# Convolution taps of one channel group on GpSimd beside the top-k, and the rotations of queries and keys after it, in a two-block sparse-attention kernel

## The reference, cut to what matters

```
proj = einsum('bld,de->ble', h, w_in[l])
a, g, zc, q, k, v, za, qi, ki, wi = split(proj)
# convolution branch: 31 taps in each of 512 channels, one after the other
u = a * sigmoid(g);  u = depthwise_conv(u, w_dw, width 31, causal) + b_dw
y_conv = silu(layer_norm(u)) * silu(zc)
# attention branch
q, k, qi, ki = apply_rope(each)               # x*cos + shifted(x)*sin
score = sum over 8 index heads of relu(qi . ki * s) * wi, causal
idx = top_k(score, 132)                       # of 528 keys, for each row
y_attn = softmax(q . k over idx) v * silu(za)
h = layer_norm(ALPHA * h + concat(y_conv, y_attn) @ w_out[l])
```

## Time and profile before

| | us |
|---|---|
| median of 3 runs | 1114.37 (1112.88 to 1114.47) |
| the profiled execution | 1111.81 |
| its span in the trace | 1110.0 |
| PE busy | 1021.1 (92%) |
| DVE busy | 697.7 (63%) |
| ACT busy | 581.6 (52%) |
| POOL busy | 130.8 (12%) |

### The profile page before, as it was taken

How to read it: one execution, slowest core, us unless ns; L and a number is a source line. 1 busy time by engine, 2 the same in 40 slices (tenths; PEclk the granted TensorE clock), 3 DMA queues, 4 the chain that set the end, 5 groups by cost and what they waited for, 6 DMA issues and landing times.

```text
span 1110.0 us, 16657 instructions
## 1 busy us (share of the span) xinstructions
PE 1021.1 (92%) x6484; PEld 868.8 (78%) x6484; DVE 697.7 (63%) x1553; ACT 581.6 (52%) x938; POOL 130.8 (12%) x185
## 2 busy tenths in 40 slices
PE   7998899778999899989989898969999999999997
PEld 7987898766677799879887666758888778877885
DVE  3999999785465559999978755562841333332522
ACT  6584781546543548458437544462484555565331
POOL 0000100101121200010001121124300000000001
PEclk9998999889899999989999989999999999999999
DMA  8775674454300767547528523295767644547661
GB/s 287 182 175 172 156 184 115 125 103 114 66 12 18 210 136 195 123 118 173 114 83 188 136 50 89 68 236 117 224 153 175 167 119 110 138 96 167 164 157 76
DMA packets 23822, 152.36 MB, mean 137 GB/s; under 512 B 2865, under 2 KB 3377, under 8 KB 6849
## 3 DMA queue, kind: packets, MB, share of 16 engines
q0 software_dynamic: 9648, 68.75, 33.4%
q1 hardware_dynamic: 14096, 82.55, 20.9%
HBM read 149.20 MB, written 2.10 MB: 136 GB/s over the span
## 4 chain that ended last, share of the span: by engine, by line
PE 77%; ACT 9%; DVE 6%; DMA 5%; issue 3%; POOL 0%; POOLq 0%; DVEq 0%; SPq 0%; ACTq 0%
PE psum_B L1176 20%; PE psum_A L1176 14%; PE psum_B L1209 9%; PE psum_A L1209 9%; PE psum_A L1330 6%; DMA w_lo<-in_weights 3%; DVE conv_acc L1626 2%; PE psum_C L1232 2%; ACT w_hi L613 2%; PE psum_B L1288 2%; PE psum_A L1542 2%; ACT w_lo L614 2%; PE psum_B L1330 2%; PE psum_B L1542 2%; DMA w_raw<-in_weights 2%
## 5 line engine op out<-in xcount | busy, mean ns | idle before, releaser
L1626 DVE SCALAR_TENSOR_TENSOR conv_acc<-u,vec,conv_acc 128x528 f32<-128x528 f32 (+1 forms) x240 | 173.4, 758 | 3.2
L1176 PE MATMUL psum_B<-x_hi,w_hi 128*128 128x264 f32 (+3 forms) x512 | 147.4, 327 | 10.7 <-ACT shifted L668 5.8
L1176 PE MATMUL psum_B<-x_lo,w_hi 128*128 128x264 f32 (+3 forms) x512 | 144.0, 320 | 0.0
L1176 PE MATMUL psum_B<-x_hi,w_lo 128*128 128x264 f32 (+3 forms) x512 | 143.4, 319 | 0.0
L1011 POOL DMA_DIRECT2D w_lo<-in_weights x67 | 59.3, 886 | 677.0 <-ACT w_lo L614 677.0
L613 ACT ACTIVATE w_hi<-w_raw 128x2048 fp32r<-128x2048 f32 (+2 forms) x87 | 129.5, 1489 | 14.3 <-DMA w_raw<-in_weights 13.9
L614 ACT ACTIVATE w_lo<-w_raw 128x2048 fp32r<-128x2048 f32 (+2 forms) x87 | 128.9, 1481 | 0.0
L1176 PE MATMUL psum_A<-x_hi,w_hi 128*128 128x264 f32 (+2 forms) x496 | 119.2, 298 | 8.2 <-DVE za L1743 4.0
L1176 PE MATMUL psum_A<-x_lo,w_hi 128*128 128x264 f32 (+2 forms) x496 | 116.8, 293 | 0.0
L1176 PE MATMUL psum_A<-x_hi,w_lo 128*128 128x264 f32 (+2 forms) x496 | 116.6, 293 | 0.0
L1176 PEld LDWEIGHTS psum_B<-x_hi,w_hi 128*128 128x128 f32 (+1 forms) x512 | 90.3, 192 | 20.0 <-issue 14.0
(11 more groups left out here) (324 smaller groups left out, 2098.0 us busy)
## 6 DMA issues: line engine op xcount, KB each, us to landing
w_raw<-in_weights SPq DMA_DIRECT2D x67, 1024.0 KB, 5.3
w_lo<-in_weights POOLq DMA_DIRECT2D x65, 1024.0 KB, 8.2
x_first<-in_x_t SPq DMA_DIRECT2D x4, 528.0 KB, 7.0
h<-in_x SPq DMA_DIRECT2D x1, 2048.0 KB, 9.8
out<-h SPq DMA_DIRECT2D x4, 512.0 KB, 2.6
post_ln_g<-in_post_ln_g SPq DMA_DIRECT2D x2, 512.0 KB, 4.2
post_ln_b<-in_post_ln_b SPq DMA_DIRECT2D x2, 512.0 KB, 5.6
w_raw<-in_weights SPq DMA_DIRECT2D x2, 288.0 KB, 5.3
```

Of the source, the lines that this page charges most:

```text
L1176: mm = pe.matmul(ps[0:cols, i, 0:b - a], w[wp][:, kt, at:at + cols], x[xp][:, kt, a:b], start=(kt == 0 and wp + xp == 0), stop=(kt == KD - ...
L1626: got = dve.scalar_tensor_tensor(dst, src, w, dst, ALU.mult, ALU.add)
```

## The change

27 of the 31 taps of group 2 go from DVE to POOL (`POOL_TAPS`). [...] They stand in POOL's order behind the selects on the scores: 3 taps at once, 5 behind the issue that follows `q` 0, 5 behind that of `q` 2, 5 behind that of `k` 0, 3 behind that of `k` 2 and 6 behind that of `v` 0. The third attention item's masked logits (L1723, `i == 2`) wait for the last of them, because they overwrite `e[2]`.

DVE keeps 97 taps: 54 before the top-k (37, then 4, 5, 5 and 3 in the index rounds), 43 with the attention items. Group 3 is no longer interleaved with group 2, but for its last four taps. The top-k runs through without the rotations, and behind the masks DVE rotates `q` 0, `k` 0, `q` 1, `k` 1, ... `k` 3. The shift buffers and ACT's waits for them stay as they were.

```diff
--- before.py
+++ after.py
@@ -219,15 +219,18 @@
     1: ((0, ("zc", 0)), (2, ("zc", 2)), (4, ("wo", 0, 0)), (6, ("wo", 1, 0)), (12, ("wo", 0, 1)), (14, ("wo", 1, 1))),
 }
 
+POOL_TAP_COUNT = 27
+POOL_TAPS = [(2, tap) for tap in range(POOL_TAP_COUNT)]
+POOL_TAPS_AFTER = {("q", 0): (3, 8), ("q", 2): (8, 13), ("k", 0): (13, 18), ("k", 2): (18, 21), ("v", 0): (21, 27)}
+
 TAPS = [(0, tap) for tap in range(11)]
 for _i in range(TAP_COUNT - 11):
     TAPS += [(0, 11 + _i), (1, _i)]
 TAPS += [(1, tap) for tap in range(TAP_COUNT - 11, TAP_COUNT)]
-TAPS += [(2, tap) for tap in range(15)]
-for _i in range(TAP_COUNT - 15):
-    TAPS += [(2, 15 + _i), (3, _i)]
-TAPS += [(3, tap) for tap in range(TAP_COUNT - 15, TAP_COUNT)]
-TAPS_AHEAD = 77
+TAPS += [(3, tap) for tap in range(TAP_COUNT - 4)]
+for _i in range(4):
+    TAPS += [(2, POOL_TAP_COUNT + _i), (3, POOL_TAP_COUNT + _i)]
+TAPS_AHEAD = 54
 TAPS_PER_ITEM = 4
 
 
@@ -493,6 +496,7 @@
         small_made = signal("small_made")
         u_made = signal("u_made")
         tap_done = signal("tap_done")
+        pool_tap_done = signal("pool_tap_done")
         rope_cos = signal("rope_cos")
         rope_sin = signal("rope_sin")
         rope_made = signal("rope_made")
@@ -519,6 +523,10 @@
                 return y_made.sem, y_made.at((use[0], "attn", use[2]))
             by = dve_took if use[1] in TAKEN_BY_DVE else act_took
             return by.sem, by.at(use)
+
+        def tap_signal(c, tap):
+
+            return pool_tap_done if (c, tap) in POOL_TAPS else tap_done
 
         items = {l: attention_items(l) for l in range(DEPTH)}
         extras = {l: attention_extras(l) for l in range(DEPTH)}
@@ -648,7 +656,8 @@
                 if name == "a":
                     if l == 1:
 
-                        act.wait_ge(tap_done.sem, tap_done.at((0, c, TAP_COUNT - 1)))
+                        last = tap_signal(c, TAP_COUNT - 1)
+                        act.wait_ge(last.sem, last.at((0, c, TAP_COUNT - 1)))
                     act.activation(pair(u[:, c, PAD:PAD + L]), ps, ACT.Copy, scale=0.5).then_inc(act_took.mark(use), 1)
                 elif name == "g":
                     buf = shift_buffer(use)
@@ -1032,6 +1041,26 @@
                                    xhi[:, c:c + CT, START[t]:END[t]].bitcast(F32), ALU.subtract) \
                     .then_inc(part_lo.mark((l, part, t)), 1)
 
+            def conv(l, first, last):
+
+                x0 = META if l else 0
+                for c, tap in POOL_TAPS[first:last]:
+                    at = V_CONVW + (l * TAP_COUNT + tap) * CT + c
+                    w = vec[:, at:at + 1]
+                    tap_src = u[:, c, tap + x0:tap + L]
+                    dst = acc[:, c, x0:L]
+                    if tap == 0:
+                        pool.wait_ge(u_made.sem, u_made.at((l, c)))
+                        b = vec[:, V_CONVB + l * CT + c:V_CONVB + l * CT + c + 1]
+                        got = pool.tensor_scalar(dst, tap_src, w, b, ALU.mult, ALU.add)
+                    else:
+                        pool.wait_ge(pool_tap_done.sem, pool_tap_done.at((l, c, tap - 1)))
+                        scaled = e[2 + tap % 2][:, x0:L]
+                        pool.tensor_scalar(scaled, tap_src, w, None, ALU.mult).then_inc(pool_step.mark((l, c, tap)), 1)
+                        pool.wait_ge(pool_step.sem, pool_step.at((l, c, tap)))
+                        got = pool.tensor_tensor(dst, dst, scaled, ALU.add)
+                    got.then_inc(pool_tap_done.mark((l, c, tap)), 1)
+
             def ln_deviation(step, t, rows):
                 pool.wait_ge(stats_made.sem, stats_made.at(step))
                 reciprocal_deviation(step, meanvar[0:rows, t, 1:2], 1, rows, t, 1.0, LN_EPS)
@@ -1062,8 +1091,11 @@
                     pool.affine_select(out=score[:, a:a + P], in_=score[:, a:a + P], compare_op=ALU.is_ge,
                                        fill=FILL, base=0, pattern=[[-1, P]], channel_multiplier=1) \
                         .then_inc(causal_done.mark((l, "score", t)), 1)
+                conv(l, 0, 3)
                 for use in USES[USES.index((l, "q", 0)):USES.index((l, "za", 0, 0))]:
                     next_blocks(use)
+                    if use[1:] in POOL_TAPS_AFTER:
+                        conv(l, *POOL_TAPS_AFTER[use[1:]])
                 for t in MAIN:
                     a = SCORE_AT[t] + START[t]
 
@@ -1295,7 +1327,8 @@
                 ps = claim(use, buf, (1,))
                 n = SIZE[t]
                 for c in range(CT):
-                    pe.wait_ge(tap_done.sem, tap_done.at((l, c, TAP_COUNT - 1)))
+                    last = tap_signal(c, TAP_COUNT - 1)
+                    pe.wait_ge(last.sem, last.at((l, c, TAP_COUNT - 1)))
                     mm = pe.transpose(ps[0:n, 0, c * P:c * P + P], acc[:, c, START[t]:END[t]], ident[:, :])
                 mm.then_inc(psum_full.mark(use), 1)
 
@@ -1622,7 +1655,8 @@
                         b = vec[:, V_CONVB + l * CT + c:V_CONVB + l * CT + c + 1]
                         got = dve.tensor_scalar(dst, src, w, b, ALU.mult, ALU.add)
                     else:
-                        dve.wait_ge(tap_done.sem, tap_done.at((l, c, tap - 1)))
+                        earlier = tap_signal(c, tap - 1)
+                        dve.wait_ge(earlier.sem, earlier.at((l, c, tap - 1)))
                         got = dve.scalar_tensor_tensor(dst, src, w, dst, ALU.mult, ALU.add)
                     got.then_inc(tap_done.mark((l, c, tap)), 1)
 
@@ -1659,7 +1693,7 @@
                         got = dve.scalar_tensor_tensor(dst, src, w, dst, ALU.mult, ALU.add)
                     got.then_inc(score_added.mark((l, hd, t)), 1)
 
-            def topk(l, between):
+            def topk(l):
 
                 rounds = -(-TOPK // 8)
                 for r in range(rounds):
@@ -1679,7 +1713,6 @@
                         vals = score[:, SCORE_AT[t]:SCORE_AT[t] + END[t]]
                         dve.wait_ge(topk_max.sem, topk_max.at((l, r, t)))
                         dve.match_replace(vals, top8[:, t - 1, :], vals, MARK).then_inc(topk_marked.mark((l, r, t)), 1)
-                    between(r)
                 for t in MAIN:
                     a, b = SCORE_AT[t], SCORE_AT[t] + END[t]
                     dve.wait_ge(topk_marked.sem, topk_marked.at((l, rounds - 1, t)))
@@ -1713,6 +1746,9 @@
                 if i >= 4:
 
                     dve.wait_ge(psum_full.sem, psum_full.at((l, "PT", *items[l][i - 4])))
+                elif i == 2:
+
+                    dve.wait_ge(pool_tap_done.sem, pool_tap_done.at((l, *POOL_TAPS[-1])))
                 a = SCORE_AT[t] if t else MASK0_AT
                 m = mask[0:n, a:a + END[t]]
                 dst = e[i % 4][0:n, 0:END[t]]
@@ -1852,21 +1888,16 @@
                     rope(l, "qi", c)
                     conv(l, (19, 24, 29, 34)[c], last)
                 rope(l, "ki", 0)
-                for i, last in enumerate((48, 59, 68, TAPS_AHEAD)):
-                    conv(l, (37, 48, 59, 68)[i], last)
+                for i, last in enumerate((41, 46, 51, TAPS_AHEAD)):
+                    conv(l, (37, 41, 46, 51)[i], last)
                     add_scores(l, 2 * i)
                     if i == 1:
                         gate_conv_input(l, 2)
                 gate_conv_input(l, 3)
-                todo = [("q", c) for c in range(CT)] + [("k", c) for c in range(CT)]
-
-                def between(r):
-                    if r > 1 and (r - 2) % 3 < 2 and todo:
-                        rope(l, *todo.pop(0))
-
-                topk(l, between)
-                for name, c in todo:
-                    rope(l, name, c)
+                topk(l)
+                for c in range(CT):
+                    for name in ("q", "k"):
+                        rope(l, name, c)
 
                 middle, todo = extras[l]["dve_middle"], extras[l]["dve"]
                 n = len(items[l])
```

## The result

The changed kernel takes 1198.99 us (median of 4 runs, 1197.62 to 1204.11), the kernel before, on the same chip, 1114.42 (1112.88 to 1114.61): 1.077 times as long, interval 1.074 to 1.080. The forecast was 1184, its range 1168 to 1202, so sign and range hold, and the loss is 84.6 us where I had 70. The forecast's own, narrower range, 1178 to 1192, was missed. The profiled execution took 1198.7, its span is 1196.9, against 1110.0, and the clock granted over the span 0.936 against 0.965.

What follows compares the result with a forecast made beforehand. PE carries 77% of the chain, so DVE's work pays only where PE waits. 1111.8 + 30.8 + 30.0 (stall and ladder) + 9 (port) = 1181.6, with 2.6 to the median 1184 us; own range 1178 to 1192, wide 1168 to 1202.

Steps and rivals of the forecast that it cites:

- The index rounds: Ahead of the top-k: with DVE's lighter rounds the top-k starts at 104.1, 12.9 us earlier; in layer 1 12.3 us earlier.
- The top-k without rotations: DVE's top-k without the eight rotations (15.8 us) takes 60.75 us; masks end at 166.0, `q` 0 is rotated at 168.1.
- the longer top-k: Sign of being wrong: MAX8 or MATCH_REPLACE8 longer than before beside POOL's taps, lengthening the wait for `q` 0.
- The stall: ACT cannot take `k` 0 until `q` 0 is rotated, so PE stands behind `k` 1 from 135.4 to 171.2.
- Rival (D): ACT is not held, PE runs its products without a gap and the index rounds pay: 1095.6 us; chance 0.05.
- The ladder: Behind the stall ACT takes one `k` per pair of rotations, 7.15 us apart; attention +30.8 us in layer 0, +30.0 in layer 1.
- The clock: Not a term of the sum; said only that PE's `k` 2, `k` 3 and `v` 0 fit between rungs, also at half clock.
- The port: POOL's taps from 175 on hold DVE's rotations by 0 to 6 us a layer; 4.5 taken, +9 us in both.
- POOL's taps: A tap on POOL takes 2.1 us (1.6 to 2.9), 27 take 57 us, hidden by the stall at no cost.
- rival (C): POOL ends last and the third attention item waits for its last tap, if taps exceed some 3.1 us: 1200; chance 0.13.
- The attention: DVE's 43 taps there in place of 47, more of them chained, cost 0, between -3 and +3 us a layer.

Runs made afterwards that it cites:

- experiment 5: The changed kernel with POOL's four selects on the scores ahead of the weight issue behind gate 3: 1196.07 us, ratio 1.072 to the kernel before.
- experiment 3: The changed kernel with four shift buffers of their own for `k` 0 to 3: 1119.55 us, ratio 1.005 to the kernel before.
- experiment 1: The kernel before with only the rotations moved behind the top-k, no taps on POOL: 1202.09 us, ratio 1.079.
- experiment 2: The changed kernel with POOL's taps 13 to 26 over 16 positions only: 1184.01 us, ratio 1.064 to the kernel before.
- experiment 10: The version with own `k` shift buffers, selects ahead and 19 POOL taps, scaling written as multiply and add of 0.0: 1097.23 us, ratio 0.985.
- experiment 6: The changed kernel with own `k` shift buffers and POOL's 27 taps regrouped 2, 4, 3, 4, 3, 11 so issues come sooner: 1123.95 us, ratio 1.008.
- experiment 4: The changed kernel with the rotations back between the rounds of the top-k: 1119.47 us, ratio 1.005 to the kernel before.

## Why the prediction was right, and where it was short

*The index rounds: right, less 2.5 us.* DVE was ready at 104.4, where I had 104.1. That the selects stand behind an issue in POOL's queue I had not followed: the issue's own wait is for ACT's split, and with DVE early that split is late. It cost 2.5 and 2.2 us; experiment 5 took out the larger part of it.

*The top-k without rotations: right.* From 106.62 to the masks at 167.34 are 60.72 us, forecast 60.75. POOL's taps lie beside only the first 40 us of it, to 147.0; but in experiment 3 they lie beside all of it, and it takes 60.73, and without any tap on POOL (experiment 1) 60.70. The Trainium skill, SBUF — State Buffer, section "Who interferes with whom", has a Vector instruction with a single SBUF input, outside its two-port modes, untouched by GpSimd; the 60.73 agree for MAX8 and MATCH_REPLACE8, and the longer top-k that the prediction had named as a sign of being wrong did not come.

*The stall: right in its mechanism and its size.* PE's wait was 37.7 us, forecast 36, and its end was ACT's L677, behind DVE's rotation. Rival (D), 1095.6, needed `k` to be free of that rotation; experiment 3 freed it and the stall went, experiment 1 shows that the stall comes with the move alone. Freeing it was not enough for (D)'s number, though: experiment 3 took 1119.6, and only with 19 taps and the issues and selects ahead was it 1097.1. By the prediction's own terms `k` 3 of layer 1 is taken at 564.7, not 564.5, which is of no weight.

*The ladder: right.* 7.24 to 7.27 in layer 0 where POOL has no taps or narrow ones (experiments 1 and 2), forecast 7.15.

*The clock: a term that I left out.* I said that PE's products fit between the rungs "also at half clock", and counted it only for `k` 2, `k` 3 and `v` 0. The first product behind the ladder, `v` 1, began at it too, on the path: 1.65 and 3.05 us. In experiments 1 and 2 that product takes 5.82 or 5.83 in both layers, behind stalls no shorter than in the changed kernel, and with 1.00 granted. So 4.2 of these 4.7 us go with the held rungs, in which PE stood longer (in layer 0 twice 3.4 us, against 0.7 and 1.4 in experiment 2); they belong to what POOL's work beside the rotations cost.

*The port: right mechanism, too small.* 6.0 and 5.9 us a layer, from experiment 2, where I took 4.5. I had one pair of rotations held. The second pair was too, since POOL's longer taps filled the time in which I had it standing at ACT's split: the rungs are 9.7 and 10.8.

*POOL's taps: the step that failed in its number.* I took 2.1 us for a tap and gave 2.9 as ceiling; it was 1.61 + 1.33 and the waits, 3.1 undisturbed, 3.4 to 4.0 beside the rotations. The ceiling rested on the thought that an operation which reads one tile less can't be longer. The nearest row, a select, was of another kind of instruction and told nothing of this one. The price is one of its form: with a second operation it is 0.71 (experiment 10). The Trainium skill, GPSIMD Engine Reference, section 3.1, has 1.8 cycles an element as the best case, which came to an estimated 0.8; the 0.71 lies somewhat below it, the form of this change at twice that, and where they differ the measurement decides. Even so rival (C) did not come: the last tap ended near 226, and the last `za` not before 237. Its condition, a tap of over some 3.1 us, was just met; but it had reckoned with an attention that asks at 231, and the attention came only at 237.

*The attention: 0 was near.* Of the 17.1 us by which the span is longer than my sum had it (1196.9 against 1179.8), 4.7 are the selects, 3 the held rotations beyond my 9, 4.7 the half clock, 4.1 the three stretches outside (0.5 + 2.9 + 0.7), and some 0.6 the rest. Why the stretch behind layer 1 is 2.9 longer I don't know; DVE's taps there are more of them chained, but no run tells that apart (with the old taps, in experiment 1, it is 1.3 longer).

*The number.* 1199 lies outside the forecast's own 1178 to 1192 and next to rival (C)'s 1200, whose mechanism did not come; it is inside the wide range by 3 us. The mechanism, the stall and the ladder, is what was right. The two terms that were too small are the port, with the clock that hangs on it, and the start of the top-k.

## What to carry to other kernels

When work is moved behind something long, list what holds its buffers, not only what needs its results: here `k` waited for `q`'s rotation by a ring of four buffers alone, and freeing it gave back 79.4 us (experiment 3 against the changed kernel). A second engine's queue is a resource like its time: its compute delays the transfers and the small steps that are issued behind it. And move only as much work as leaves the engine that sets the end alone: with free buffers 27 taps lost 0.5 to 0.8% (experiments 3 and 6), and 19, with the selects ahead, won 1.6%.

## What the hardware showed that I had not expected

GpSimd's `tensor_scalar` over 128x528, with nothing beside it that lengthens it, takes 1.61 us with a multiply alone and 0.71 with multiply and add; the first tap, a multiply and add with two values from a tile, takes 1.09. The form with less to do is the slowest; why, no run shows. No more than these three forms was measured, and only in float32.

The hold between DVE and POOL goes both ways and depends on the pair: a rotation's operation rose from 0.70 to 1.83 us, POOL's scaling from 1.61 to 1.94 and at most to 2.48, while rounds of MAX8 and MATCH_REPLACE8 kept their pace. A single input does not always spare an operation: DVE's mask of 128x144 (L1720, a `tensor_scalar` from float32 to bf16) took 0.23 us in the kernel before and 1.40 in experiment 4, where it began beside a POOL addition. (A scaling just behind a weight issue shows some 1.9 us with no rotation beside it, as at 114.95 in the changed kernel; that is not this hold.)
